# A weight ring of three slots, re-dealt modulation steps and one set of squares for two norms, in a kernel that streams 595 MB of weights

## The reference

```
first_block:  x += concat(pool(u), hgrn2(q, f, i, g)) @ w_out      # [u q f i g] = rmsnorm(x) @ w_in
              x += cross_attention(rmsnorm(x), rmsnorm(mem), wq, wk, wv) @ wo
              x += experts(rmsnorm(x))                             # top group, top 2 of 4 experts in it
              x  = rmsnorm(x, norm_final)
second_block: for l in 0, 1:
                shift, scale, gate = silu(c) @ w_ada_2[l] + b_ada_2[l]
                h = rmsnorm(x, norm_g_2[l]) * (1 + scale) + shift
                z = h @ w_in_2[l]                                  # 13 pieces of 512 columns
                y = concat(fourier, neighbourhood attention, retention, conformer conv)(z) @ w_out_2[l]
                x = x + gate * y
              return rmsnorm(x, final_g)
```

## Time and profile before

| | us |
|---|---|
| median of 3 runs | 2083.03 (2081.29 to 2087.2) |
| profiled execution, device time | 2087.8 |
| its span | 2085.9 |
| PE busy | 2037.2 (98%) |
| DVE busy | 1750.0 (84%) |
| ACT busy | 1196.9 (57%) |
| mean granted TensorE clock | 0.991 |

### The profile page before, as it was taken

How to read it: one execution, slowest core, us unless ns; L and a number is a source line. 1 busy time by engine, 2 the same in 40 slices (tenths; PEclk the granted TensorE clock), 3 DMA queues, 4 the chain that set the end, 5 groups by cost and what they waited for, 6 DMA issues and landing times.

```text
span 2085.9 us, 42604 instructions
## 1 busy us (share of the span) xinstructions
PE 2037.2 (98%) x18977; PEld 1641.7 (79%) x18977; DVE 1750.0 (84%) x1662; ACT 1196.9 (57%) x1079; POOL 57.0 (3%) x72
## 2 busy tenths in 40 slices
PE   8999999999999999999999999999999999999998
PEld 7889888888889955555556568888888888888887
DVE  7785687998887788999999999989877789898755
ACT  5553644454444578887877864456554454555543
POOL 0002300000000000000000000010000000100000
PEclk9999999999999999999999999999999999999999
DMA  8854577789888878999999987765758776557552
GB/s 302 298 202 165 180 289 271 287 293 329 317 319 300 298 300 343 420 420 420 420 420 413 416 320 277 257 197 190 282 189 302 270 290 245 194 197 275 200 202 102
DMA packets 96742, 595.27 MB, mean 285 GB/s; under 512 B 11176, under 2 KB 11336, under 8 KB 37808
## 3 DMA queue, kind: packets, MB, share of 16 engines
q1 hardware_dynamic: 94912, 583.66, 74.6%
q0 software_dynamic: 1648, 8.90, 1.2%
HBM read 588.32 MB, written 2.10 MB: 283 GB/s over the span
## 4 chain that ended last, share of the span: by engine, by line
PE 73%; DVE 13%; DMA 8%; ACT 3%; issue 2%; DVEq 0%; POOL 0%; ACTq 0%; POOLq 0%
PE GB L2256 54%; PE GB L2685 6%; DVE w_lo L1303 5%; PE MB L2685 4%; DVE W L1303 3%; DMA raw<-w_up 2%; ACT w_hi L653 2%; DMA Z<-w_ada 2%; DMA W<-w_ada 2%; DMA raw<-w_down 1%; DVE W L1274 1%; DMA raw<-w_gate 1%; DVE Z L1274 1%; PE MB L2843 1%; PE MB L2480 1%
## 5 line engine op out<-in xcount | busy, mean ns | idle before, releaser
L653 ACT ACTIVATE w_hi<-raw 128x2048 f16<-128x2048 f32 x308 | 588.1, 1910 | 697.2 <-PE GB L2256 673.6
L1303 DVE SCALAR_TENSOR_TENSOR w_lo<-raw,w_hi 128x2048 f16<-128x2048 f32 x308 | 706.1, 2294 | 236.8 <-ACT w_hi L653 235.5
L2256 PE MATMUL GB<-H,w_hi 128*128 128x256 f16 x4352 | 721.7, 274 | 16.5 <-DVE w_lo L1303 11.6
L2256 PE MATMUL GB<-H,w_lo 128*128 128x256 f16 x2176 | 595.4, 274 | 0.0
L2256 PEld LDWEIGHTS GB<-H,w_hi 128*128 128x128 f16 x4352 | 422.9, 98 | 82.8 <-DVE w_lo L1303 16.3
L2256 PEld LDWEIGHTS GB<-H,w_lo 128*128 128x128 f16 x2176 | 213.7, 98 | 25.4
L1274 DVE SCALAR_TENSOR_TENSOR W<-W,SM 128x1024 f32<-128x1024 f32 x150 | 192.2, 1281 | 35.6 <-DMA W<-w_ada 31.6
L2256 PE MATMUL GB<-w_hi,H 128*128 128x256 f16 x1280 | 210.8, 273 | 0.0
L2256 PE MATMUL GB<-w_lo,H 128*128 128x256 f16 x640 | 174.4, 273 | 0.0
L2256 PE MATMUL GB<-Z,w_hi 128*128 128x256 f16 x1024 | 170.0, 274 | 4.0 <-DVE w_lo L1303 4.0
L2256 PE MATMUL GB<-W,w_hi 128*128 128x256 f16 x1024 | 168.0, 273 | 1.8 <-DVE w_lo L1303 1.8
(11 more groups left out here) (487 smaller groups left out, 2751.2 us busy)
## 6 DMA issues: line engine op xcount, KB each, us to landing
raw<-w_in SPq DMA_DIRECT2D x144, 1024.0 KB, 5.4
W<-w_ada SPq DMA_DIRECT2D x160, 512.0 KB, 5.7
raw<-w_out SPq DMA_DIRECT2D x48, 1024.0 KB, 5.4
raw<-w_down SPq DMA_DIRECT2D x41, 1024.0 KB, 10.3
raw<-w_gate SPq DMA_DIRECT2D x34, 1024.0 KB, 11.7
raw<-w_up SPq DMA_DIRECT2D x32, 1024.0 KB, 12.8
raw<-xattn_wk SPq DMA_DIRECT2D x16, 1024.0 KB, 5.1
raw<-xattn_wq SPq DMA_DIRECT2D x16, 1024.0 KB, 7.6
```

Of the source, the lines that this page charges most:

```text
L653: act.activation(w, raw_at[r], ACT.Copy, scale=W_SCALE).then_inc(hi_done, 1)
L1303: dve.scalar_tensor_tensor(lo, raw_at[r], W_SCALE, hi, ALU.mult, ALU.subtract).then_inc(raw_taken[r], 1)
L2256: last = pe.matmul(o, a, m, start=first, stop=end and w_part is lo, skip_group_check=True)
```

## The change

- The ring has three slots (`SPL = 3`). The third one is raw room 3, read as fp16 (`third`); the other two keep `w_hi` and `w_lo`. Room 3 serves as a raw room only for expert blocks 4 to 185, room 7 now until the experts' end. ACT and DVE may write the parts of block m when PE has finished block m-3.
- SP puts the loads of a block's modulation steps behind the load of the next block, not of the one after that (`load_due(1)`).
- In `halves` the last steps of the first set are at blocks 9, 10, 10, 11 instead of 10, 12, 14, 16, and the second set is at blocks 38 to 47. The taps are dealt anew.
- In `z0` and `z1` split 3 on DVE stands at the end of `shifted_parts`, ahead of the steps of blocks 2 and 3.
- PE runs blocks 0 and 1 of `z0` and `z1` together (`first_blocks`): for each unit of x first the products with its high part in both blocks, then those with its low part; for the last two units first block 0 and then block 1.
- At the experts' end `SQG`, its squares and DVE's adds are gone. A small tile `TWO` holds ones and norm_final², and `two_sums(c)` multiplies the squares of chunk c by both columns at once: chunks 0 to 7 inside steps 90 and 91, 8 to 11 behind the loop ahead of the last unsorting, 12 to 15 behind it. Split 0 of `z0` moves ahead of the last output's high part on ACT and of the last unsorting's add on DVE.

```
-SPL = 2
+SPL = 3
-        open_ = list(range(RAW))
+        open_ = list(range(RAW - 1))
         if 0 <= j < n:
-            open_ += [4] * (j >= 6) + [5] * (7 <= j < 126) + [6] * (j >= 7) + [7] * (13 <= j < 150)
+            open_ += [3] * (4 <= j < 186) + [4] * (j >= 6) + [5] * (7 <= j < 126) + [6] * (j >= 7) + [7] * (j >= 13)
...
-        for m in [2, 2, 3, 4, 4, 5, 6, 6, 7, 8, 8, 9, 10, 12, 14, 16]:
+        for m in [2, 2, 3, 4, 4, 5, 6, 6, 7, 8, 8, 9, 9, 10, 10, 11]:
             put(ph, m)
-        for m in [35, 36, 37, 37, 38, 39, 39, 40, 41, 41, 42, 42, 43, 44, 45, 46]:
+        for m in [38, 38, 39, 39, 40, 40, 41, 41, 42, 42, 45, 45, 46, 46, 47, 47]:
             put(ph, m)
...
+        third = raw[:, RAW - 1, :].bitcast(F16)
+        hi_of = [w_hi[:, 0, :], w_hi[:, 1, :], third[:, 0:BLK]]
+        lo_of = [w_lo[:, 0, :], w_lo[:, 1, :], third[:, BLK:2 * BLK]]
...
-                        load_due(2)
+                        load_due(1)
...
-                if m > 2 or ph not in K_MAJOR:
+                if m > 2 + (ph in ("z0", "z1")) or ph not in K_MAJOR:
                     modulation(ph, m)
...                                              # end of shifted_parts on DVE
                     if k == 6:
                         split(ph, 2)
+                split(ph, 3)
...                                              # DVE, z0 and z1
                 for m in range(4 * PIECES):
-                    if m >= 3:
+                    if m >= 4:
                         split(ph, m)
-                    elif m == 2:
+                    elif m >= 2:
                         modulation(ph, m)
...                                              # PE, z0 and z1
+            def first_blocks(ph, hi, lo):
...
+                for n in range(n_units):
+                    early = n < n_units - 2
+                    pe.wait_ge(S("norm_hi"), hi + n + 1)
+                    for u in range(2 if early else 1):
+                        unit(n, u, False)
+                    pe.wait_ge(S("norm_lo"), lo + n + 1)
+                    for u in range(2 if early else 1):
+                        ins = unit(n, u, True)
+                ins.then_inc(block_done[s[0] % SPL], 1)
+                for n in range(n_units - 2, n_units):
+                    unit(n, 1, False)
+                    ins = unit(n, 1, True)
+                ins.then_inc(block_done[s[1] % SPL], 1)
...                                              # PE, experts' end
+            def two_sums(c):
+                for a in range(TT):
+                    ins = pe.matmul(GB[:, 0, 2 * a:2 * a + 2], SQ[:, c, a * P:a * P + P], TWO[:, c, :], start=c == a == 0, stop=c == KC - 1,
+                                    skip_group_check=True)
+                return ins
...
+                        if MOE_STEPS - 6 <= n < MOE_STEPS - 4 and k % 2:
...
+                            two_sums(4 * (n - MOE_STEPS + 6) + 2 * c + k // 2)
```

More of the change, by code:

```diff
@@ L940, in _ @@
             act.activation(upper_h[:, :], const("upper"), ACT.Copy)
+            act.activation(TWO[:, :, 0], ones[:, 0:KC], ACT.Copy)
+            act.activation(TWO[:, :, 1], col("norm_final", 0, KC), ACT.Square)
             def pair_squares(p, ph="wo"):
@@ L1029, in _ @@
                         place_turned()
+                    if n == MOE_STEPS - 1 and part == 1:
+                        split("z0", 0)
                     if ending and n < MOE_STEPS - 1:
@@ L1058, in _ @@
                         act.wait_ge(S("un_add"), e // 2)
-                        if c == 8:
-                            given_up(act, 7)
                         act.activation(SQ[:, c:e, :], XT[:, c:e, :], ACT.Square).then_inc(S("sq"), 1)
[L1062 to L1065, removed]
                     if n + 2 < MOE_STEPS:
                         split("moe", 2 * n + 4 + part)
-            split("z0", 0)
             split("z0", 1)
[L1070 to L1075, removed]
+            act.wait_ge(S("un_add"), 7)
+            act.activation(SQ[:, 12:14, :], XT[:, 12:14, :], ACT.Square).then_inc(S("sq"), 1)
             token_root(4, two_var, two_root)
@@ L1950, in _ @@
                         link(dve.tensor_tensor(GAIN[:, :], GAIN[:, :], col("norm_final", 0, KC), ALU.mult))
[L1951 to L1958, removed]
-                            dve.tensor_tensor(sq[:, 0:2, :], sq[:, 0:2, :], sq[:, 2:4, :], ALU.add).then_inc(S("sq_add"), 1)
                     if n + 2 < MOE_STEPS:
                         split("moe", 2 * n + 4 + part)
+            split("z0", 0)
             unsort_add(3, 0)
-            split("z0", 0)
             unsort_add(3, 1)
@@ L2277, in block, with unit @@
                 product(ph, m, u, 8 * k, k == 0, k == 1, groups, x, rows, between).then_inc(block_done[s % SPL], 1)
+            def first_blocks(ph, hi, lo):
+                n_units = sum(u[0] < 8 for u in UNITS)
+                s, parts = [where(ph, u)[1] for u in range(2)], []
+                for u in range(2):
+                    taken(pe, ph, u)
+                    pe.wait_ge(bank_free[u], uses[ph][u])
+                    parts.append([w[slot(s[u])].rearrange("p (c n) -> p c n", c=8) for w in (hi_of, lo_of)])
+                def unit(n, u, low):
+                    w_hi, w_lo = parts[u]
+                    for k in UNITS[n]:
+                        for x, w in ((xl, w_hi),) if low else ((xh, w_hi), (xh, w_lo)):
+                            for half in range(2):
+                                ins = pe.matmul(GB[:, u, half * T:half * T + T], w[:, k, half * P:half * P + P], x[:, k, :],
+                                                start=k == 0 and half == 0 and w is w_hi and not low, stop=False, skip_group_check=True)
+                    return ins
[12 more added lines that the diff above has]
+                ins.then_inc(block_done[s[1] % SPL], 1)
             def spare(n, o):
@@ L2699, in _ @@
                             unsort(f - 9, c)
[L2700 to L2702 removed]
+                        if MOE_STEPS - 6 <= n < MOE_STEPS - 4 and k % 2:
+                            if n == MOE_STEPS - 6 and c == 0 and k == 1:
+                                pe.wait_ge(S("moe_lo"), LO_AT["y"] + 12)
+                                pe.wait_ge(S("sq"), SQ_AT["two"] + 1)
+                            two_sums(4 * (n - MOE_STEPS + 6) + 2 * c + k // 2)
+            pe.wait_ge(S("sq"), SQ_AT["two"] + 2)
+            for c in range(8, 12):
+                two_sums(c)
+            spare(1, GB[:, 3, 0:P])
             unsort(3, 0)
             unsort(3, 1)
[L2705 to L2708 removed]
+            spare(2, GB[:, 3, 0:P])
+            pe.wait_ge(S("sq"), SQ_AT["two"] + 3)
+            two_sums(12)
+            two_sums(13)
+            pe.wait_ge(S("sq_add"), ADD_AT["two"] + 1)
+            two_sums(14)
+            two_sums(15).then_inc(S("norm_ms"), 1)
+            spare(7, GB[:, 3, 0:P])
             spread_root(2, r_all)
@@ L2884, in _ @@
                         small(f"pw{l}", ca, MB[:, 0:2, :])
-                    block(ph, m, ready=("norm_lo", *range(17 + 9 * l, 26 + 9 * l)), rows=Z_ORDER[m // 4] in (4, 8))
+                    if m == 0:
+                        first_blocks(ph, 16 + 9 * l, 16 + 9 * l)
+                    elif m > 1:
+                        block(ph, m, ready=("norm_lo", *range(17 + 9 * l, 26 + 9 * l)), rows=Z_ORDER[m // 4] in (4, 8))
                 for m in range(16):
```

68 lines of the change are left out of this document (28 added, 40 removed).

## The result

| | before | changed |
|---|---|---|
| median, us | 2085.1 (4 runs) | 2099.4 (4 runs, 2095.3 to 2101.7) |
| ratio, 95% interval | | 1.0068 (1.0048 to 1.0087) |
| profiled execution / its span | 2087.8 / 2085.9 | 2095.25 / 2093.4 |
| from the start of block 2 to that of block 12, us: `z0`, `mix0`, `z1` | 55.79, 54.54, 55.15 | 65.07, 52.40, 65.20 |

The medians differ by 14.3 us; the forecast was 21.7. The profiled execution of the changed kernel is the lowest of its four and only 7.5 us of span above the profiled one of before.

What follows compares the result with a forecast made beforehand. PE, 98% busy, was taken as the bound, with the two staging buffers' round trip as second resource. Terms -2.3 - 0.6 - 1.6 + 1.9 + 11.1 + 11.2 + 2 = +21.7 gave 2104.7 us on the median, range 2078 to 2115.

Steps and rivals of the forecast that it cites:

- `w_in`, ring: In w_in, the ring of three gives back 0.6 us of PE's stalls; nothing to 4.4 held possible.
- `z0` from block 2 to 13: In z0, late steps 13 to 15 and DVE work ahead of split 12 delay block 12 by 11.1 us.
- `z1` from block 2 to 13: In z1, the same delay of block 12, 10.2 us, plus 1.0 for the clock: +11.2.
- late steps, both phases: Sixteen steps in pairs at blocks 38 to 47 outrun the round trip: +1 us a phase, +2 in all.
- The start of the steps: In z0, split 3 ahead of step 0 makes it start 3.2 us later, some 6 behind block 2.
- The pace: In z0 and z1, two staging buffers keep the steps at 3.51 and 3.49 us each, as before.
- The clock: In z1, a lower granted clock behind a stall of over 3 us adds 1.0 us.
- Experts: At the experts' end, 16 added fp32 matmuls cost 4.0 us, partly given back: net +1.9.
- A: Rival: loads arrive in time, regularly under 4 us, and DVE's work alone counts: -10, some 2073 us; chance 0.14.
- B: Rival: pace holds, only the late start costs, +6.4 and +6.6 in z0 and z1: about 2092 us; chance 0.13.
- C: Rival: three rooms starve the ring in the attention's projections, +24 less overlap: about 2127 us; chance 0.05.
- D: Rival: parts cancel, the ring returning the late start's 3 us in each phase: 2083 us; chance 0.12.

Runs made afterwards that it cites:

- moe_only: The kernel before with only the experts' end changed (sums inside steps 90 and 91, split 0 of z0 earlier): 2084.7 us, ratio 0.9997.
- before_new_plan: The kernel before with only the new lists of steps and taps, ring of two and four raw rooms kept: 2096.7 us, ratio 1.0054.
- ring_only: The kernel before with only the ring of three, three raw rooms outside the experts and load_due(1): 2076.6 us, ratio 0.9965.
- four_buffers: The changed kernel with four staging buffers instead of two for the 16 early steps of z0 and of z1: 2075.9 us, ratio 0.9957.
- both_back_four: The changed kernel with lists and split 3 undone and four staging buffers for the early steps of z0 and z1: 2073.2 us, ratio 0.9945.
- both_back: The changed kernel with the lists of steps and taps and the place of split 3 both undone, all else kept: 2077.1 us, ratio 0.9966.
- before_four: The kernel before with four staging buffers for the early steps of z0 and z1, all else as before: 2084.2 us, ratio 0.9998.

## Why the prediction was right, and where it was off

The mechanism and both of its places were right; the sum overshot. It was made for the profiled pair, where 21.7 stands against 7.5; against the medians it is 21.7 and 14.3, and the width of the range did its part. By its own terms, with the profiled pair (first block of each stage, changed minus before; by `moe_only` above, a term of one window can be some 2 us off):

| term | forecast | measured |
|---|---|---|
| `w_in`, ring | -0.6 | -1.8 |
| attention, ring | -2.3 | -2.5 |
| experts' end and norm, up to block 2 of `z0` | +1.2 | +0.5 |
| `z0` from block 2 to 13 | +11.8 | +9.8 |
| `mix0` | -1.6 | -2.1 |
| norm ahead of `z1` | -0.7 | -0.8 |
| `z1` from block 2 to 13 | +11.9 | +10.0 |
| late steps, both phases | +2.0 | -1.5 |
| slow blocks of before that are absent | 0 | -5.0 |
| ahead of the first matmul, and behind the last block | 0 | +0.9 |

*The start of the steps.* Forecast 6.1 us behind block 2, measured 6.10; behind step 14 the forecast had 12.3 to block 12, measured 1321.68 - 1309.2 = 12.5. *The pace* was the mis-sized term: I carried 3.51 and 3.49 over from the kernel before, and measured 3.32 in `z0` ((1309.2 - 1262.71)/14) and 3.25 in `z1`. At that pace step 14 comes 2.6 and 3.4 us earlier, against windows that are 2.0 and 1.9 shorter than forecast; the rest went the other way, in `z0` 0.2 behind step 14 and a stall of 0.5 at block 13, in `z1` the clock.

Why the pace was faster: before, the even steps 2 to 12, which make the chain, started 0.22 us (`z0`) and 0.05 us (`z1`) after their loads had landed, in the changed kernel 0.04 and 0.05. So waiting for a place in DVE's list accounts for half of the difference in `z0` and for none in `z1`. The rest is the loads of that chain: in the mean 5.58 and 5.71 us before, 5.37 and 5.19 in the changed kernel (steps 2 to 14), and half of such a difference goes into each step. It comes with the new lists and not with the ring: from step 0 to step 12 of `z1` the three kernels with new lists and two buffers, `before_new_plan` with its ring of two among them, take 3.17 to 3.21 us a step, six others with the old lists and two buffers 3.49 to 3.57. The load's length, which I took as given, depends on the order of the rest; that it is shorter because PE, held up, asks for fewer blocks meanwhile (275 GB/s in `z0` against 302) is my guess, which no run separates.

*The clock* cost more in `z1` than the 1.0 that I had set: 1.7 us in the block at 1691.44 and 2.6 in that at 1735.24, and the second delays block 12 in full. In `z0`, where a stall of 3.11 us fell in one piece too, it cost nothing (see the last section).

*Late steps.* I costed the pairs at blocks 38 to 47 at +1 a phase; they cost nothing, and three small stalls of before (0.1, 0.1 and 0.5 a phase) are gone, in `ring_only` as well, so by the ring. *`w_in`.* I gave back 0.6 of the 4.4 us of stalls; 1.8 went here and all 4.4 in the profile of `ring_only`. But `before_new_plan`, whose `w_in` is that of before, is 1.7 shorter there too (slow blocks set apart), so these profiles do not fix what the ring gives in `w_in`. *Experts.* The 16 added matmuls are there and a little dearer than forecast (8.8 us for 64 records, 0.138 each, so 4.4 for 32, where I had 4.0), but `moe_only` puts the whole edit between -2.7 and +1.7, so what I costed at +1.9 had cover that I did not see. Where it lies stays open: the stretch before is held by transfers and moved by 1 us and more between kernels that are alike there.

*Slow blocks.* Before, three blocks of 6.92 us followed stalls of 2 to 3 us, in `w_in` (two) and `w_out`; in the profiled execution of the changed kernel the stalls in their places, 2.1 to 2.2 us, are followed by 5.25 (stalls from start to start). That is 5.0 us, and with it the profiled pair would differ by 12.5, near the 14.3 of the medians. Not the ring: the profile of `before_new_plan`, which has the same kernel there as before, lacks two of the three as well. Over the 14 profiles the block behind the idle 1.94 us in `w_in` took 6.92 in six and 5.25 in seven (in one the idle time was shorter), and the one behind 2.05 in `w_out` 6.92 in five and 5.25 in nine. It differs from execution to execution, and a stall of this length is a draw for 1.7 us.

*Rivals.* A's condition (loads regularly under 4 us) was not met: of the 26 loads of steps 2 to 14 in the two phases two are under 4. But A's bound for `z0`, 56.0 by DVE's work alone, was near once the buffers were there (57.0 measured). The prediction read 3.73 as the shortest load of the trace; that is the shortest of the rows shown, and the shortest of all 192 took 3.2 us before and 3.4 in the changed kernel. By the Trainium skill (SBUF — State Buffer, The DMA setup-cost knee) a load of this size is an estimate of 3.2 us. The traces agree for the shortest loads alone; the medians are 5.7 and 5.6. (Two buffers would allow a step each 2.2 us by it, not the 2.3 written.) B, only the late start, was too small by 6 us of the median (its own sum is +10.4, so 2093 rather than 2092). The windows alone tell less against it: 9.3 and 10.1 us longer, where its +6.4 and +6.6 with the 0.7 of an earlier block 2 make 7.1 and 7.3. C, the three rooms, cost nothing in the attention: `ring_only` is faster. D's return by the ring is real (7 us) but not in the phases that lose.

## What to carry to other kernels

A chain of load, use, free, next load has a rate of its own, (load + use)/buffers, with the load as long as it takes beside the others; before work is moved into fewer blocks, compare that rate with the blocks' rate, and if it is slower add buffers first: here the same order of work cost +14 us with two and gave -9 with four. An item put ahead of the first link delays every link. In an in-order list of transfers, a prefetch must not stand behind a wait that ends later than its own: when the number of rooms goes down, the lookahead has to go down with it, and when a chain is spread out, look for its consumer first.

## What the hardware showed that I had not expected

The load of half a megabyte took from 3.65 to 8.91 us within 20 us of one phase, 5.6 in the median of the whole run, at a DMA share of 0.78 in that stretch. I take it to be what else is in flight. What the runs show of that: with four buffers, where more loads are under way at once, those into `Z` took 7.7 in the median (`four_buffers`) and 7.4 (`both_back_four`) instead of 5.4 and 5.9 with two (the changed kernel and `both_back`). With the ring of two the difference is small, 6.1 against 6.0 (`before_four`).

The granted clock fell behind stalls of only 2 to 3 us in some executions and not in others (6.92 or 5.25 for the same block behind the same stall of 2.10), and behind the stall of 4.13 it was 0.66 over the next block. The length of the stall alone does not decide: in the changed kernel it stayed at 1.00 over the block behind a stall of 3.11.

```profile
1315.39 0.39 PE L2254 MATMUL GB<-H,w_hi 128*128 128x256 f16 x2 [3.11 <-DVE w_lo L1306]
```

```profile
1315.39:1320.60 5.21, 5.21 (x48) 4.62 (x48) 5.17 (x9) 2.86 (x2) 0.00 (x0) 1.00 0.70 244
```
